# An eleventh expert tile in a two-layer decoder trunk, its sixteen expert pairs written out, and its buffers laid out anew

## What is computed

```
h    = rmsnorm(x, norm1_g)
proj = h @ w_in                       # 1024 -> 2824 columns
y_m  = chunkwise mLSTM on 4 heads     # after a causal convolution and SiLU of q, k
y_a  = causal softmax attention on 8 heads, QK-norm, partial rotary
y_s  = S5 state space scan in 16 groups, GELU, then a GLU (glu_w)
x    = x + concat(y_m, y_a, y_s) @ w_out
# mixture of experts
h    = rmsnorm(x, norm2_g)
group  = argmax(h @ w_group)          # 1 of 4 groups
top 2 of the 8 experts in that group, weights from both softmaxes
x    = x + sum over the 2 experts of weight * (silu(h@w_gate) * (h@w_up)) @ w_down
```

## Time and profile before

| | |
|---|---|
| median of 3 runs | 1297.69 us |
| the profiled execution's own time | 1291.37 us |
| its span | 1289.6 us |
| granted TensorE clock, mean | 0.927 |
| PE busy | 1070.8 us (83%) |
| DVE busy | 460.6 us (36%) |
| ACT busy | 179.9 us (14%) |
| moved by DMA | 440.56 MB, mean 342 GB/s |

### The profile page before, as it was taken

The page is one execution under the profiler, slowest core; times in us unless marked ns, Lnnn a source line. Parts: engine busy times, 40 slices in busy tenths (PEclk is TensorE's granted clock), DMA queues, the critical chain, the costliest instruction groups (busy, mean ns, idle before and its releaser), DMA issues.

```text
span 1289.6 us, 23165 instructions
## 1 busy us (share of the span) xinstructions
PE 1070.8 (83%) x9476; PEld 576.8 (45%) x9477; DVE 460.6 (36%) x1253; ACT 179.9 (14%) x427; POOL 23.7 (2%) x36
## 2 busy tenths in 40 slices
PE   5999999997887766776799999898767777679966
PEld 3476654453333333333355755543333333334433
DVE  0786445433232222222237753533222222224321
ACT  2224310010010000000024160100000000001000
POOL 3000002000000000000000000000000000000000
PEclk8999999998998888888899999998888888889988
DMA  9621378999999999999993313799999999996997
GB/s 313 228 104 66 137 296 288 383 427 426 426 427 427 426 427 426 426 427 427 387 332 140 131 66 131 326 376 427 426 424 427 428 426 428 425 426 277 428 428 297
DMA packets 50270, 440.56 MB, mean 342 GB/s; under 512 B 9313, under 2 KB 11521, under 8 KB 25089
## 3 DMA queue, kind: packets, MB, share of 16 engines
q1 hardware_dynamic: 48112, 435.79, 81.7%
q0 software_dynamic: 960, 1.51, 0.7%
q10 hardware_dynamic: 1104, 1.85, 0.5%
HBM read 437.56 MB, written 1.05 MB: 340 GB/s over the span
## 4 chain that ended last, share of the span: by engine, by line
PE 52%; DMA 41%; DVE 3%; issue 2%; DVEq 1%; ACT 0%; SPq 0%; ACTq 0%
DMA ring<-in_e_w_up_dram 24%; PE PS L1462 12%; DMA ring<-in_e_w_down_dram 9%; PE PS L1525 8%; DMA ring<-in_e_w_gate_dram 7%; PE PS L1499 6%; PE PS L1761 4%; PE PS L1519 3%; PE PS L1424 3%; PE PS L1415 3%; PE PS L1434 2%; DMA gT<-in_norm_g_dram 1%; PE PS L1695 1%; PE PS L1715 1%; PE PS L1475 1%
## 5 line engine op out<-in xcount | busy, mean ns | idle before, releaser
L1462 PE MATMUL PS<-ring,hT 128*32 128x256 f32 x4608 | 336.5, 452 | 171.6 <-DMA ring<-in_e_w_gate_dram 112.4
L1462 PEld LDWEIGHTS PS<-ring,hT 128*32 128x32 f32 x4608 | 182.6, 125 | 347.0 <-issue 283.4
L1499 PE MATMUL PS<-ring,hT 128*32 128x512 f32 x1152 | 137.1, 618 | 11.5 <-DMA ring<-in_e_w_down_dram 11.5
L874 DVE TENSOR_SCALAR hT<-hT 128x256 f32<-128x256 f32 x36 | 10.6, 294 | 334.1 <-ACT hT L607 334.1
L1525 PE MATMUL PS<-ring,hT 128*128 128x512 f32 x256 | 113.1, 595 | 0.0
L1424 PE MATMUL PS<-cst,mixT 64*64 64x64 f32 x1216 | 81.2, 282 | 5.8 <-ACT mixT L602 1.4
L1424 PEld LDWEIGHTS PS<-cst,mixT 64*64 64x64 f32 x1216 | 77.1, 212 | 15.0 <-issue 11.8
L1415 PE MATMUL PS<-xres,scr 128*64 128x512 f32 x304 | 73.6, 605 | 0.0
L1499 PEld LDWEIGHTS PS<-ring,hT 128*32 128x32 f32 x1152 | 36.4, 113 | 82.7 <-issue 80.8
L1434 PE MATMUL PS<-hT 64*128 64x512 f32 x288 | 71.8, 615 | 0.0
L1525 PEld LDWEIGHTS PS<-ring,hT 128*128 128x128 f32 x256 | 47.5, 190 | 53.6 <-issue 53.6
(11 more groups left out here) (342 smaller groups left out, 898.4 us busy)
## 6 DMA issues: line engine op xcount, KB each, us to landing
ring<-in_e_w_gate_dram SPq DMA_DIRECT2D x64, 2048.0 KB, 38.6
ring<-in_e_w_up_dram SPq DMA_DIRECT2D x64, 2048.0 KB, 39.8
ring<-in_e_w_down_dram SPq DMA_DIRECT2D x60, 2048.0 KB, 37.3
ring<-in_w_in_dram SPq DMA_DIRECT2D x10, 2048.0 KB, 18.5
ring<-in_w_out_dram SPq DMA_DIRECT2D x2, 4096.0 KB, 13.0
ring<-in_e_w_down_dram SPq DMA_DIRECT2D x8, 1024.0 KB, 38.7
ring<-in_w_in_dram SPq DMA_DIRECT2D x2, 1024.0 KB, 23.2
xres<-in_x_dram ACTq DMA_DIRECT2D x1, 1024.0 KB, 9.9
```

The costliest lines, as they stand in the source:

```text
L1462: last = pe.matmul(PS[o:o + UT, bank, 0:256], xTe[:, k, UT * u:UT * u + UT], w[u][:, k, :, 2 * h:2 * h + 2], start=k == 0, stop=k == KD - 1)
L1499: last = pe.matmul(PS[o:o + UT, 3, :], hTe[:, c % 2, hc:hc + UT], w[u][:, c, 512 * h:512 * h + 512], start=c == 0, stop=c == KF - 1)
```

## The change

It has four parts.

1. `NTILE` goes from 10 to 11. The buffer `flat` is one piece of 11 x 4096 + 8 + 512 floats per partition. Tile 10 starts 8 floats behind its regular place. Over tile 10 lie, outside the expert stage, `vm`, `so`, `gluw`, the head selectors `sel` (once columns of the constants), `uT` and six of the eight blocks of `mixT`; the other two lie behind the tile. Values of the router that the expert stage needs (`wgt`, `sh`, `sw`) go to `small`, as do the rows of parameters. The constants shrink from 1481 to 969 columns.
2. SP's loop and TensorE's loop over five pairs are written out as 16 pairs. Addresses and counts become constants, and TensorE's waits for tiles too.
3. Matrix n now lies in tile n % 11 and waits for matrix n-11. In the mixer stage SP loads 1, 2, 3, then 0, 6, 4 and 5, 7, 8 and 9 at the places where it loaded 0, 1, 2, 8, 5, 3 and 4, 9, 6 and 7. Matrix 10 comes after the plan.
4. The input chunks go to tiles 8, 9, 0, 1, 2, 3, and the working buffers to other tiles. The GLU weights and the selectors are loaded by SP behind the chunks, in a parameter group of their own (3).

```diff
-NTILE = 10
+NTILE = 11
 TILE = 4096
+GAP = 8
...
+        flat = sb("ring", [P, NTILE * TILE + GAP + 2 * T])
+
+        def tile(t, o=0, n=TILE):
+
+            a = TILE * t + (GAP if t == NTILE - 1 else 0) + o
+            return flat[:, a:a + n]
...
+        late = NTILE * TILE + GAP
+        mixT = flat[:, late - 6 * T:late + 2 * T].rearrange("p (k t) -> p k t", k=KD)
+        gluw = over(10, 1024, (2, T))
+        sel = over(10, 2048, (MH, P))
+        vm = flat[:, TILE * (NTILE - 1):TILE * (NTILE - 1) + NT * MH * (HD + 1)]
+        so = over(10, 512, (NT, T))
+        uT = over(10, 1536, (2, Q, NCH))
...
-            t = (6, 7, 8, 0, 1, 2)[c]
-            return ring[:, t, 0:KD * w].rearrange("p (k n) -> p k n", k=KD)
-
-        wout = flat[:, 6 * TILE:8 * TILE].rearrange("p (k n) -> p k n", k=KD)
+            t = (8, 9, 0, 1, 2, 3)[c]
+            return tile(t, 0, KD * w).rearrange("p (k n) -> p k n", k=KD)
+
+        wout = flat[:, 8 * TILE:10 * TILE].rearrange("p (k n) -> p k n", k=KD)
...
-            par(gluw[:, :, :], at(s_glu_w, l).rearrange("l (c p) n -> (l p) c n", p=P), 1)
+            par(gluw[:, :, :], at(s_glu_w, l).rearrange("l (c p) n -> (l p) c n", p=P), 3)
+            par(sel[0:MH, :, :].rearrange("p h n -> p (h n)"), consts[0:MH, C_SEL:C_SEL + MH * P], 3)
...
                 wait_apart(sp, s_ctl, l + 1)
+                load_matrix(l, 10)
                 if not last:
                     load_small(sp, l + 1, (0,))
...
-                with sp.Fori(0, 2) as i5:
-                    for n in range(NTILE, NTILE + 30):
-                        if n % 2 == 0:
-                            tile_free(n, i5)
-                        load_matrix(l, n, i5 * 5)
-                for n in range(NTILE + 60, NLOAD):
-                    if n % 2 == 0:
-                        tile_free(n)
+                def tile_free(n):
+
+                    m = n - NTILE
+                    if m % 2 == 0:
+                        c = C_PASS + 1 + m // 6
+                        done = sp.value_load(ctl[0:1, c:c + 1], min_val=1, max_val=L * MAXN)
+                        wait_apart(sp, s_used[kind_of(m)], done)
+
+                for n in range(NTILE, NLOAD):
+                    tile_free(n)
                     if n < NLOAD - 2:
                         load_matrix(l, n)
...
-                    for c, n in enumerate((96, 97, 98, 100, 101, 102)):
-                        if n % 2 == 0:
-                            tile_free(n)
+                    for c, n in enumerate((96, 97, 99, 100, 101, 102)):
+                        tile_free(n)
                         load_chunk(c, l + 1)
+                    load_small(sp, l + 1, (3,))
...
-            act.dma_start(cst[:, :], consts).then_inc(s_cst, 16)
+            act.dma_start(cst[:, :], consts[:, 0:NC]).then_inc(s_cst, 16)
...
-                        wait_apart(pe, s_tile[t], i5 * 48 + count)
-                        yield ring[:, t, :]
+                        pe.wait_ge(s_tile[t], count)
+                        yield tile(t)
...
-                with pe.Fori(0, NPAIR // 5) as i5:
-                    for i in range(5):
-                        expert_pair(i, i5)
-                expert_pair(NPAIR - 1, 0)
+                for i in range(NPAIR):
+                    passes = pe.value_load(ctl[0:1, C_NP + i:C_NP + i + 1], min_val=1, max_val=MAXN // 2)
+                    past_n = pe.value_load(ctl[0:1, C_PASS + i:C_PASS + i + 1], min_val=0, max_val=L * MAXN)
+                    with pe.Fori(0, passes) as q:
+                        one_pass(l, past_n + q, i)
```

More of the change, by code:

```diff
@@ L58 @@
 C_SIN = C_COS + NT * 8
[L59 to L60 removed]
+C_GID = C_SIN + NT * 8
 C_P = C_GID + NE
@@ L113, in sem, with over @@
             return ctx.enter_context(nc.semaphore(name))
-        ring = sb("ring", [P, NTILE, TILE])
-        flat = ring[:, :, :].rearrange("p q n -> p (q n)")
-        def over(tile, o, shape):
+        flat = sb("ring", [P, NTILE * TILE + GAP + 2 * T])
+        def tile(t, o=0, n=TILE):
+            a = TILE * t + (GAP if t == NTILE - 1 else 0) + o
+            return flat[:, a:a + n]
+        def over(t, o, shape):
             n = math.prod(shape)
@@ L123, in over @@
             sizes = {f"x{i}": n for i, n in enumerate(shape)}
-            return ring[:, tile, o:o + n].rearrange(f"p ({names}) -> p {names}", **sizes)
+            return tile(t, o, n).rearrange(f"p ({names}) -> p {names}", **sizes)
         cst = sb("cst", [P, NC])
         xres = sb("xres", [P, NT, D])
-        xs = over(9, 0, (NT, D))
+        xs = over(7, 0, (NT, D))
         hT = sb("hT", [P, KD, T])
-        mixT = sb("mixT", [P, KD, T])
-        rows = mixT[0:R_DT, 4, 0:P]
-        ldt = mixT[0:ST, 5, 0:2 + P]
+        late = NTILE * TILE + GAP
+        mixT = flat[:, late - 6 * T:late + 2 * T].rearrange("p (k t) -> p k t", k=KD)
+        small = sb("small", [P, 330])
+        rows = small[0:R_DT, 72:200]
+        ldt = small[0:ST, 200:202]
+        ldts = mixT[0:ST, 5, 0:P]
         pc = sb("pc", [P, NR])
@@ L159, in build @@
[L159 to L164 removed]
+        conv = over(5, 0, (4, T + 3))
+        cA = over(5, 1036, (2, ST, Q + 1, 32))
+        tab = over(4, 0, (2, ST, NQ))
+        qkm = over(4, 1088, (4, T))
+        xst = over(4, 2112, (2, ST, NCH))
+        decay4 = over(4, 3136, (ST, NCH))
+        pm = over(4, 3648, (384,))
@@ L165, in build @@
+        s5p = over(0, 0, (4, ST, NCH))
+        s5w = over(0, 2048, (2, ST, NCH))
+        ydir = over(0, 3072, (512,))
+        silu = over(4, 2112, (1024,))
+        hsq = over(4, 2112, (512,))
+        vlog = over(0, 3584, (512,))
+        osq = over(0, 2048, (512,))
+        prob = over(0, 0, (2, 512))
+        probT = over(0, 1024, (2, 512))
+        vm = flat[:, TILE * (NTILE - 1):TILE * (NTILE - 1) + NT * MH * (HD + 1)]
         v65 = vm[:, :].rearrange("p (j h d) -> p j h d", j=NT, h=MH)
-        so = sb("so", [P, NT, T])
+        so = over(10, 512, (NT, T))
@@ L208, in build @@
         s_gain = sem("gains_in")
-        s_par = [sem(f"{k}_in") for k in ("rows", "s5_and_head_weights", "router_weights")]
-        NPAR = (10, 9, 4)
+        s_par = [sem(f"{k}_in") for k in ("rows", "s5_and_head_weights", "router_weights", "glu_weights_and_selectors")]
+        NPAR = (10, 8, 4, 2)
         s_win = [sem(f"w_in_{c}") for c in range(6)]
@@ L503, in _, with load_matrix @@
         def _(sp):
-            def load_matrix(l, n, pairs_on=0):
+            def load_matrix(l, n):
                 t = n % NTILE
-                sp.dma_start(ring[:, t, :], we_v[kind_of(n)][bass.ds(pairs_on * 2 + (l * NE + expert_of(n)), 1)][0]
-                             ).then_inc(s_tile[t], 16)
+                sp.dma_start(tile(t), we_v[kind_of(n)][l * NE + expert_of(n)]).then_inc(s_tile[t], 16)
             def load_chunk(c, l):
@@ L1486, in one_pass @@
                         pe.wait_ge(s_half[u], 16 * l + 16)
-                    w = [ring[:, (NLOAD - 2 + u) % NTILE, :].rearrange("p (k n) -> p k n", k=KF) for u in range(2)]
+                    w = [tile((NLOAD - 2 + u) % NTILE).rearrange("p (k n) -> p k n", k=KF) for u in range(2)]
                 else:
@@ L1729, in _ @@
                 vo_part(2)
-                parameters(pe, 1, l)
+                parameters(pe, 3, l)
                 pe.wait_ge(s_z, l + 1)
```

88 lines of the change are left out of this document (30 added, 58 removed).

## The result

The kernel after the change takes 1279.18 us (median of 4 runs, 1275.59 to 1279.57) against 1297.53 for before (4 runs, 1295.09 to 1298.72): ratio 0.9853, 95% interval 0.9833 to 0.9873, 18 to 19 us faster. A repetition gave 0.9832 (0.9795 to 0.987). The forecast was 1282.2 with a lower end of 1279.0. The ratio applied to the 1297.69 of the forecast gives 1278.6, 3.6 us under the forecast and just outside the range: faster, and by about a fifth more than the forecast's 15.5 us. The interval reaches back into the range. (In the rows PE is TensorE, SP the engine whose queue asks for the tiles, ACT ScalarE, DVE VectorE and POOL GpSimd.)

What follows compares the result with a forecast made beforehand. DMA tile streaming at about 426 GB/s bounds the expert stages, so idle DMA gaps cost time. Expert stages 4.9 + 4.9 + 4.9 = 14.7, plus start 0.8, give 15.5 us: 1297.7 - 15.5 = 1282.2 us, own range 1279 to 1285.

Steps and rivals of the forecast that it cites:

- start: Kernel start: 256 KB less constants ahead of x and the gains brings the first product forward 0.8 us, bounds 0 and 1.6.
- gap (d): Layer 1's threefold pair, ring full, 10.4 us idle DMA: PE's release also moves, a second 4.9 us, bounds 0 and 4.9.
- Gap (a): Layer 0 after the plan, 5.5 us idle DMA: tile 10 loads there, 4.9 us gained, bounds 3.9 and 4.92.
- (b): Layer 0, 240 to 247 us, ring full, 2.9 us idle DMA: absorbs up to 1 us lateness of earlier requests.
- Gap (c): Layer 1 after the plan, 8.8 us idle DMA: tile 10 loads there, 4.9 us gained.
- The sixteen pairs: Writing out the pair loops removes PE's 5.74 and 7.46 us issue idles, covered by the tile stream: worth 0.
- D: Rival: the jumps' 13.2 us of issue idle show in the time as well, 1269 us; chance 0.03.
- Tile 10's place: Starting 32 bytes past a multiple of 4096 floats costs 0; other bound 8 us, transaction-rule estimate 1.2 us.
- C: Rival, slower: tile 10 is written or read slowly for its odd place; 1302 us at 25%, 1361 at half speed; chance 0.05.
- E: Rival: tile 10 moves at only 387 GB/s, 8 us lost, 1290.2 us; chance 0.07.
- A: Rival: the threefold pair's second gain is lost, or layer 0's lateness is not absorbed; 1287.1 us; chance 0.17.
- B: Rival: the tile fills nothing, small loads and something unseen take the gaps; 1296.9 us; chance 0.04.

Runs made afterwards that it cites:

- b_all: Before with ten tiles plus pairs written out, smaller constants and GLU weights loaded behind the chunks; 1290.19 us, ratio 0.9956 to before.
- a_late10: After, but SP asks for matrix 10 only after pair 0's gate product, not right after the plan; 1283.5 us, ratio 0.9893 to before.
- a_pool_loop: After with 3024 one-element memsets on POOL behind layer 0's plan, as a loop of 12 rounds; 1275.24 us, ratio 0.9836 to before.
- a_gap64: After with tile 10 moved from 8 to 64 floats behind its regular place; 1280.51 us, ratio 0.9873 to before.
- a_warm2: After with two unused extra TensorE products ahead of each layer's last up product; ratio 0.9853 to before.
- a_gain1: After with the first norm's gains loaded ahead of x on ACT's queue; 1280.57 us, ratio 0.9876 to before.
- b_same1: Before, unchanged, profiled once more; 1296.3 us.
- b_unroll: Before with only TensorE's and SP's loops over five pairs written out as sixteen pairs; ratio 0.9982 to before.
- b_pe: Before with only TensorE's loop over five pairs written out; ratio 0.9991 to before.
- b_sp: Before with only SP's loop over five pairs written out; ratio 1.0007 to before.
- a_warm: After with four unused extra TensorE products ahead of each layer's last up product; ratio 0.9873 to before.
- a_pool_line: After with 3024 one-element memsets on POOL behind layer 0's plan, written out as straight code; 1285.37 us, ratio 0.9914 to before.
- b_cst: Before with only the smaller constants, the selectors loaded later by SP; ratio 0.9993 to before.
- b_glu: Before with only the GLU weights moved from POOL's queue to behind SP's chunks; ratio 0.9987 to before.
- b_same2: Before, unchanged, a third profiled execution; 1298.61 us.

## Why the prediction was right, and where it was wrong

With three executions of before and two of after (after, a_again) the spans average 1293.6 and 1274.9, 18.7 us apart, as the medians. The stage means of these five share it out:

| term | forecast | measured | from |
|---|---|---|---|
| start | 0.8 | 2.1 | F0: 20.0 to 17.9 |
| mixers | 0 | 1.7 | 367.7 to 366.0, the clock |
| layer 0, g to F1 | 4.9 | 6.8 | 450.9 to 444.1 |
| layer 1, g to u | 9.8 | 9.2 | 435.0 to 425.8 |
| u to end | 0 | -1.1 | 20.0 to 21.1, last up product at half clock |
| sum | 15.5 | 18.7 | |

Two terms came out larger than forecast beyond the spread of equal kernels, the written-out pairs and the start, and one smaller, gap (d). Luck has a part in how far the whole is off: the mixers' 1.7 and the end's -1.1 are the clock of single executions, and without them the sum is 18.1, 1279.6 us, just inside the range.

**Gap (a) and (b), 4.9: right.** From the first gate to the 12th product b_all has 103.2 us and after 97.1. Of these 6.1, 1.2 is b_all's first gate at half clock (5.06 against 3.83 us), which leaves 4.9. The lateness of gap (a) was taken up by (b), as argued: of b_all's 4.3 us idle there after leaves 1.8. From the 12th product on the two are equal (326.03 both).

**Gap (c), 4.9: right.** 68.1 us in b_all, 68.3 in a_late10, 63.4 in after: 4.7 to 4.8. What remains idle is 3.1 us.

**Gap (d), 4.9: right in mechanism, 3.3 in size.** The step was that PE's release moves as far as its tiles. PE in after at the threefold pair:

```profile
1128.18 3.86 PE L1468 MATMUL PS<-ring,hT 128*32 128x256 f32 x64 [1.28 <-DMA ring<-in_e_w_up_dram]
...
1138.07 5.27 PE L1505 MATMUL PS<-ring,hT 128*32 128x512 f32 x32 [1.24 <-issue]
...
1157.38 3.64 PE L1505 MATMUL PS<-ring,hT 128*32 128x512 f32 x32
1160.84 3.83 PE L1468 MATMUL PS<-ring,hT 128*32 128x256 f32 x64
```

and in a_pool_loop:

```profile
1130.32 3.83 PE L1477 MATMUL PS<-ring,hT 128*32 128x256 f32 x64 [1.83 <-DMA ring<-in_e_w_up_dram]
1140.07 3.64 PE L1514 MATMUL PS<-ring,hT 128*32 128x512 f32 x32 [1.14 <-issue]
```

The first down product of this pair took 5.27 us in after (5.31 in a_again, 5.25 in a_gap64) and 3.64 where the clock stayed full (a_pool_loop, a_late10). The up product moved from 1142.31 to 1128.18, 14.1 us, and the release from 1177.36 to 1165.14, 12.2. The stage column (d) tells the price: 124.5 in the three with the half clock, 122.6 to 123.3 in a_late10, a_warm2, a_gain1 and the two POOL kernels, against 127.8 before. At full clock the term is 4.5 to 5.2. At half clock it is the same: the one ten-tile execution whose down product fell there too (b_same1, 5.07 us) has 129.2, 4.7 more than 124.5. The missing 1.6 us is the 5.27 less 3.64. The gap ends when PE has done its third gate product, so what the clock takes from that down product comes out in the gap's end. The clock fell there in three of the nine eleven-tile executions; why is not shown.

**The sixteen pairs, 0: this step failed.** PE's two idles of 5.7 and 7.5 us were covered by the tile stream, and D, which gave them 13.2 us, is wrong. The prediction asked which engine waits at the jump and not what else the jump does. b_unroll is 2.3 us faster than before (0.3 to 4.5), and b_pe and b_sp say that it is TensorE's loop. In layer 0's saturated part the kernels without the jump have 326.0 to 326.2 us (a_warm and a_pool_line aside) and the six with it 327.5 to 328.8: 1.4 to 2.8. From layer 1's first gate to its 8th product b_unroll and b_pe have 66.8 against b_same1's 67.7, all three with a first gate at full clock: 0.9 (with one at half clock b_all has 68.1 against 68.8 to 69.2). Together 2.3 to 3.7 us for a term that was put at nothing.

By what way the jump costs this is shown in part. In layer 0 it arises behind the second jump back: at the 25th product, the first of the eleventh pair, which waits for its tiles, b_pe, b_unroll and b_all stand 167.9 to 168.0 us behind the 12th product and the six with the jump 169.3 to 170.7. Instruction packets are the likely cause, since a_pool_line shows that extra ones can hold up the tiles, and this part has four of TensorE's fewer without the jump. But they don't account for layer 1. Its two jumps back lie between its 8th and 24th product. There the kernels without them have 13 such packets and those with them 16 to 18, and the time is the same: 237.6 to 238.0 against 237.9 to 238.4. The 0.9 us lie ahead of the 8th product, where no jump back has run yet and all have six packets. So the written-out loop saves 2 to 4 us, and the share of the packets in it stays open.

The Trainium skill, "Runtime: NRT & Kernel Launch", section "Instruction fetch mechanics", has the sequencer fetch its pages by a DMA queue of its own and calls the cost of crossing a page mostly hidden. For the engine that fetches, the trace agrees: POOL, with 22 packets more, idled 11.8 us on "issue" among its memsets in the straight version and 10.7 in the loop. The tile stream felt them all the same: a_pool_line has 0.29 us for each of them.

**The start, 0.8: this term was mis-sized, 2.1.** It was priced as 256 KB at the rate of all queues together. For x that holds: in b_cst it came 0.8 us sooner than in before (10.40 and 11.23). But the first product waits for the gains as well, and they came at least 2.4 us sooner, so that DVE then waited for the transposes of x and no longer for them. Before, then the two rows of b_cst:

```profile
11.23 3.65 PE L1402 MATMUL PS<-cst,xres 128*128 128x128 f32 x16 [11.23 <-DMA xres<-in_x_dram]
```

```profile
10.40 3.65 PE L1406 MATMUL PS<-cst,xres 128*128 128x128 f32 x16 [10.40 <-DMA xres<-in_x_dram]
14.18 1.29 DVE L841 TENSOR_TENSOR hT<-PS,gT 128x512 f32<-128x512 f32 x2 [13.25 <-PE PS L1406]
```

The queue's own rate doesn't explain it: over 2 to 8 us ACT's queue moved 1.52 MB in before, 253 GB/s, at which 256 KB are 1.0 us. Why the small gain loads behind x gained more than twice that stays open. b_cst shows 2.4 us for the constants alone, above even my bound of 1.6. b_glu's 1.1 adds only 0.25 to it (b_all 17.32), since in b_cst DVE's first product waits for x's transposes already. These single starts vary by about 1 us (17.27 in after, 18.59 in a_again), so 2.1 is good to that.

**Tile 10's place, 0: right** (a_gap64), and C and E with it are wrong: the saturated windows run at 427 GB/s. The prediction's 1.2 us came from a rule on bytes fetched, while tile 10 is written at its odd place, so a_gap64 says nothing of fetching from such a place.

**The clock.** The last up product of both layers fell to half clock: 5.43 us in layer 0 and 5.45 in layer 1, against 3.87 and 3.88 in before's profile. The tiles at the end of layer 0 came 10.1 us sooner (634.99 to 624.91), the next layer began 8.5 sooner. In ten-tile kernels it falls in one or both as well (b_same1, b_same2, b_pe, b_unroll, b_all), and in a_late10 and the two POOL kernels in neither, so this is no sure effect of the change, but it was lost in both layers in after, a_again and a_gap64. The 1.7 us of the mixers point the other way. Six ten-tile executions with before's mixers (before, b_same1, b_same2, b_sp, b_pe, b_unroll) spread from 365 to 374 us there, so it can't be said whether the new places have a part in it.

**The range** was too narrow at its lower end: 15.5 with nothing for the jumps, and an own range that held the start's 1.6 but no gain from the written-out code. The rivals: A, B, C, D, E did not come. Of the tile that A takes from gap (d) a third was lost, by the clock and not by its mechanism.

No experiment beat after beyond its variation: a_warm2 1276.95, a_pool_loop 1275.24 (two runs) and a_again 1277.37 lie together.

## What to carry to other kernels

Where the DMA engines are the bound, count everything that goes through them, instruction pages too: a loop that jumps back over a long body may cost something although the engine's own stall is covered, and so may long straight code on an engine that nobody waits for. In this kernel a buffer more was worth its transfer time once in each gap in which the ring was full or the next tile not yet asked for, and where PE sets the gap's end, its clock decides whether the whole is kept. Before a forecast is laid over one profiled execution, look how its clock compares with that of the timed ones: here 0.927 against 0.918, the median of 33 timed executions of before.

## What the runs showed of the hardware

- 22 instruction packets of 8.2 KB more for POOL (a_pool_line against a_pool_loop) went with tiles complete 6.3 us later, 0.29 us each, while all engines together moved the same 426 to 427 GB/s, as if they all passed one of the 16 engines.
- TensorE's jumps back over five pairs: it idled 5.7 to 7.5 us at those that the tiles didn't cover, four 16 KB packets more passed in layer 0's saturated part, and that part was 1.4 to 2.8 us longer. In layer 1 three to five more packets went with no longer time.
- A saturated stream onto a tile that starts 32 or 256 bytes past a multiple of 16 KB in the buffer, in 16 KB pieces, took the same time within 0.2 us a stage.
- 256 KB less ahead of the first needed loads in one queue brought x 0.8 us forward and the first product, which waits for the small gains behind x, 2.4 us (b_cst against before, one execution each), while 335 GB/s flowed over all queues.
- The same kernel's mixers took 365 to 370 us in three executions, with the granted clock over them 0.97 and 1.00 in the shortest and 0.95 and 0.99 in the longest.
